# Moving one Gram product behind the chunk outputs, swapping three PSUM banks, and clamping a norm one slot later

## The chip, the cores and the metric

The kernel runs on one core of a Trainium2 chip. The metric is the device time of one execution in microseconds; of several executions the median is taken. TensorE is called PE, VectorE DVE, ScalarE ACT, GpSimd POOL, and the queue that issues most transfers SP.

## The reference

Two transformer-like blocks are applied to a sequence of 512 tokens of width 1024, in float32. The change touches only one part of the first block: a linear recurrence with 8 heads of 64 channels, run forwards and backwards over the tokens.

```python
def rwkv7_scan(r, w, k, v, kk, a, reverse):
    def step(state, inp):
        r_t, w_t, k_t, v_t, kk_t, a_t = inp
        sa = jnp.einsum('bhij,bhj->bhi', state, -kk_t)
        state = (state * w_t[:, :, None, :]
                 + sa[..., None] * (kk_t * a_t)[:, :, None, :]
                 + v_t[..., None] * k_t[:, :, None, :])
        y_t = jnp.einsum('bhij,bhj->bhi', state, r_t)
        return state, y_t
...
    kk = (k * k_k.astype(f32)).reshape(B, S, H, N)
    kk = kk / jnp.maximum(jnp.sqrt(jnp.sum(kk * kk, axis=-1, keepdims=True)), 1e-12)
...
    y = (rwkv7_scan(r_h, decay[:, :, 0], k_dir[:, :, 0], v_h, kk, a[:, :, 0], False)
         + rwkv7_scan(r_h, decay[:, :, 1], k_dir[:, :, 1], v_h, kk, a[:, :, 1], True))
```

Around it stand an input projection, a differential attention, gates, output projections, a feed-forward network, and a whole second block; none of these is edited.

## The kernel before

The recurrence is computed in chunks of 64 tokens, by `rwkv_block`. A pair is 128 channels, so two heads; there are four pairs (`RT = 4`), one after the other, and for each both directions `d` = 0 and 1 are worked on side by side. A pair goes through these stages, in which every engine has its own written-out order:

1. Gram products. `gram_l(p, d)` multiplies within each chunk (32 matmuls) into PSUM: direction 0 into pair 3 (banks 6 and 7), direction 1 into pair 2 (banks 4 and 5). DVE then runs `begin(p, d)`: four instructions (L1363, L1365, L1367, L1369), whose last one gives `X`, on which PE's next stage waits (semaphore `x0`). DVE runs `begin` for direction 0, then for direction 1, and only then the rest.
2. Inversion in five levels by doubling, in banks 0 and 1 (bank `d` for direction `d`). A level has two rounds: PE multiplies (L1090, semaphore `m1`), DVE masks into `E` (L1409), PE multiplies again (L1103, semaphore `px`), ACT copies out (L1273), DVE transposes (L1421). Between the rounds stand slots 0 to 9 of `beside(p, slot)` with other work: on PE the second Gram products of this pair in slots 1 and 2, with their masks on DVE (L1379, L1380), and `prepare(p + 1, n)`, the preparation of the next pair.
3. Right sides, then the run over the chunks: seven steps. A step is two matmuls per direction (L1161) into bank 4 + d, and one DVE instruction per direction (L1451, semaphore `zout`). In the same stretch PE sums those parts of the output that do not need the state (L1170) into banks 0 and 1, and transposes the next pair's operands (L1018).
4. At the end of a pair PE does `gram_l(p + 1, 0)` and `gram_l(p + 1, 1)`, then the output part that needs the states (64 matmuls, L1187, again into banks 1 and 0), and ACT copies the two banks out (L1295, semaphore `yo`). PE waits for both copies before level 1 of the next pair.

Among all this, PE also does 128 tiles of a gate projection in bank 3, three matmuls each (L839, L840, L841). `Gates.STEPS` says how many tiles stand at each point of the order: two at the end of a pair (behind L1187), none at slot 0, two at slot 1, one at slot 2. DVE scales the finished gate tiles (L869) and splits their weights (L854).

The preparation that the second edit touches goes through bank 2 and passes from engine to engine. Step 1: PE sums squares over a head (L985, semaphore `kksum`). Step 2: DVE clamps the sum from below (L1314, semaphore `kkmax`), and PE waits for that before its next product in the same bank (L988, semaphore `lora`), which ACT turns into a sigmoid (L1204) ahead of its next copies L1273. PE has this product at slot 2, behind the second Gram product of direction 1 and ahead of one gate tile and of L1103 of level 2. DVE has the clamp at slot 1:

```python
                    if p + 1 < RT:
                        if slot != 2:
                            prepare(p + 1, slot)
                        if slot == 1:
                            prepare(p + 1, 2)
```

The functions below are printed whole, with the profile's line numbers.

Of the kernel before, what the change touches and what calls it, by code (L numbers as in the profile page):

```python
# [885 lines left out]
def rwkv_block(pr, U, w_lora, room, spare, gates, back, room_free, earlier):  # L886
# [4 lines left out]
    with ExitStack() as ctx:  # L891
# [63 lines left out]
        with nc.Block() as block:  # L955
# [17 lines left out]
            def _(pe):  # L973
# [60 lines left out]
                def gram_l(p, d):  # L1034

                    if d == 0:
                        pe.wait_ge(s["trout"], 6 * p + 5)
                    elif p:
                        pe.wait_ge(s["zout"], 14 * p)
                    gram(p, d, "Bh")  # L1040

                def times_v(p, d):
# [34 lines left out]
                gates.pe(pe, 19)  # L1077
                for p, point in enumerate(pair_points):
                    if p:
                        pe.wait_ge(s["yo"], 2 * p)  # L1080
                    for lev in range(1, 6):
                        u = 5 * p + lev - 1
                        for d, a in both(p):
# [67 lines left out]
                    for i in range(NCH - 1):  # L1151
                        for d, a in both(p):
                            at = ORDER[d][i]
                            if i == 0:
                                pe.wait_ge(s["phiout"], 2 * p + d + 1)
                                pe.wait_ge(s["zero"], 2 * p + d + 1)
                                pe.wait_ge(s["psiout"], 4 * p + 2 * d + 2)
                            else:
                                pe.wait_ge(s["zout"], 14 * p + 2 * (i - 1) + d + 1)
                            for hh in range(2):  # L1160
                                last = nc.tensor.matmul(pr.bank[4 + d][rows64(hh), (i % 4) * 64:(i % 4 + 1) * 64],  # L1161
                                                        a["Phi"][rows64(hh), 4 * (at % 2) + at // 2, :], a["Z"][rows64(hh), at, :],
                                                        start=True, stop=True)
                            last.then_inc(s["step"], 1)
                        for b, hh, d, a, k in fixed_parts[5 * i:5 * (i + 1)]:
                            q, h = hh * TB + b, rows64(hh)
                            for cc in range(2):
                                r = rows64(cc)
                                left, right = ((vN[r, b, h], a["A2"]), (a["N"][r, q, 0:64], a["A1"]))[k]
                                last = nc.tensor.matmul(pr.bank[1 - cc][h, 64 * b:64 * b + 64], left, right[r, q, :],  # L1170
                                                        start=(b == 0 and d == 0 and k == 0), stop=False, skip_group_check=True)
                        if i == 6:
                            last.then_inc(s["fixed"], 1)
                        gates.pe(pe, point + 12 + i)
                        if i and p + 1 < RT:
                            transposes(p + 1, i - 1)
                    if p + 1 < RT:
                        for d in range(2):
                            gram_l(p + 1, d)
                    pe.wait_ge(s["rbout"], 2 * p + 2)  # L1180
                    pe.wait_ge(s["zout"], 14 * p + 14)
                    pe.wait_ge(s["fixed"], p + 1)
                    for b in range(TB):
                        for cc in range(2):
                            for d, a in both(p):
                                for hh in range(2):
                                    last = nc.tensor.matmul(pr.bank[1 - cc][rows64(hh), 64 * b:64 * b + 64],  # L1187
                                                            a["Z"][rows64(hh), 2 * b + cc, :],
                                                            a["Rb"][rows64(hh), (2 * b + cc) * CH:(2 * b + cc + 1) * CH],
                                                            start=False, stop=(d == 1), skip_group_check=True)  # L1190
# [4 lines left out]
            def _(act):  # L1195
# [70 lines left out]
                for p, point in enumerate(pair_points):  # L1266
                    for lev in range(1, 5):
                        u = 4 * p + lev - 1
                        beside(p, 2 * lev - 2)
                        gates.act(act, point + 2 * lev - 2)  # L1270
                        for d, a in both(p):
                            act.wait_ge(s["px"], 2 * u + d + 1)
                            nc.scalar.copy(flat(a["X"][:, :, :]), pr.bank[d]).then_inc(s["xout"], 1)  # L1273
                        beside(p, 2 * lev - 1)
                        gates.act(act, point + 2 * lev - 1)
                    beside(p, 8)
                    gates.act(act, point + 8)
                    for d, a in both(p):
                        act.wait_ge(s["y5"], 2 * p + d + 1)
                        nc.scalar.copy(flat(a["Y64"][:, :, :]), pr.bank[d]).then_inc(s["y64"], 1)  # L1280
                    gates.act(act, point + 9)
                    for d, a in both(p):
                        act.wait_ge(s["n"], 2 * p + d + 1)
                        act.wait_ge(s["gram"], 4 * (p + 1))
                        nc.scalar.mul(a["N"], pr.pair[2 + d][:, :].rearrange("p (q t) -> p q t", q=8), -1.0).then_inc(s["nout"], 1)
                    beside(p, 9)
                    for i in range(10, 13):
                        gates.act(act, point + i)
                    for i in range(6):
                        gates.act(act, point + 13 + i)  # L1290
                        if p + 1 < RT:
                            transposed(p + 1, i)
                    act.wait_ge(s["y"], p + 1)
                    for cc in range(2):
                        nc.scalar.copy(U[:, p, :].rearrange("p (b cc t) -> p b cc t", b=TB, cc=2)[:, :, cc, :],  # L1295
                                       pr.bank[1 - cc][:, 0:256].rearrange("p (b t) -> p b t", b=TB)).then_inc(s["yo"], 1)
                    gates.act(act, point + 19)

            @block.vector
            def _(dve):  # L1300
# [70 lines left out]
                def beside(p, slot):  # L1371
                    if slot == 0:
                        for d, a in both(p):
                            nc.vector.tensor_tensor(by_head(a["A1"][:, :, :]), gram_part(d, 0), by_token(incl, d), ALU.mult)\
                                .then_inc(s["a1"], 1)
                    if slot in (1, 2):
                        d, a = both(p)[slot - 1]
                        dve.wait_ge(s["gram"], 4 * p + slot + 2)
                        nc.vector.tensor_tensor(by_head(a["M"]), gram_part(d, 1), by_token(strict, d), ALU.mult).then_inc(s["m"], 1)  # L1379
                        nc.vector.tensor_tensor(by_head(a["A2"][:, :, :]), gram_part(d, 0), by_token(incl, d), ALU.mult).then_inc(s["a2"], 1)  # L1380
                    if p + 1 < RT:
                        if slot != 2:
                            prepare(p + 1, slot)
                        if slot == 1:
                            prepare(p + 1, 2)
                    if slot == 8:
                        bonus(p)

# [15 lines left out]
                for p, point in enumerate(pair_points):  # L1404
# [40 lines left out]
                    for i in range(NCH - 1):  # L1445
                        for d, a in both(p):
                            at, nxt = ORDER[d][i], ORDER[d][i + 1]
                            dve.wait_ge(s["step"], 14 * p + 2 * i + d + 1)
                            if i == 0:
                                dve.wait_ge(s["psiout"], 4 * p + 2 * d + 2)  # L1450
                            nc.vector.scalar_tensor_tensor(a["Z"][:, nxt, :], pr.bank[4 + d][:, (i % 4) * 64:(i % 4 + 1) * 64],  # L1451
                                                           a["pin"][:, at, CH * (1 - d):CH * (1 - d) + 1], a["Z"][:, nxt, :],
                                                           ALU.mult, ALU.add).then_inc(s["zout"], 1)
                        gates.dve(dve, point + 12 + i)
                        if i == 0:
                            dve.wait_ge(s["rb"], 2 * p + 2)
                            order = "p (b cc t) -> p cc b t"
                            for d, a in both(p):
                                nc.vector.tensor_tensor(a["Rb"].rearrange(order, b=TB, cc=2), a["Rt"].rearrange(order, b=TB, cc=2),
                                                        heads_of(pr.pair[3], 256 * d), ALU.add).then_inc(s["rbout"], 1)  # L1460
# [1541 lines left out]
```

## Time and profile before

| quantity | value |
|---|---|
| median of three executions | 1845.11 us (1844.65 to 1846.07) |
| the profiled execution, its own time | 1846.07 us |
| its span, from the first to the last instruction | 1844.3 us |
| PE busy | 1733.6 us (94%) |
| DVE busy | 1052.2 us (57%) |
| ACT busy | 706.6 us (38%) |
| mean granted PE clock over the span | 0.982 |

The profile is of one execution. The busy time of PE includes the time a matmul takes to pass through, so a busy PE is not PE at its peak. A row of the order of instructions gives the start in the span, the duration, the engine, the source line, the tensors, the shapes and how many instructions were merged into the row; in brackets stand the idle time of the engine before it and what ended that.

### The profile page before, as it was taken

Reading aid. Unit: us, or ns where it says so; the run is one execution under the profiler, and the core shown is the slowest. Engines: PE = TensorE matmul, PEld = TensorE weight load, DVE = VectorE, ACT = ScalarE, POOL = GpSimd, SP = SyncE. Lnnn points to the kernel's source line nnn. Section 1 sums busy time; section 2 is a strip of 40 time slices with the busy share of each in tenths; the row PEclk is TensorE's granted clock in tenths of the full one; section 3 lists DMA queues with packets and bytes.
Section 4 is the critical chain, followed back from the end, with each engine's and each line's share of the span. In section 5 each row is a group of like instructions: output and inputs, shape, how many; then the busy total and the mean of one; then the engine's idle time right before and its main releaser. Section 6 shows DMA issues by size and latency. Waiting matters only on the chain. (4 is left out here: it accounts for less than half of the span.)

```text
span 1844.3 us, 29753 instructions
## 1 busy us (share of the span) xinstructions
PE 1733.6 (94%) x12674; PEld 1357.3 (74%) x12674; DVE 1052.2 (57%) x1461; ACT 706.6 (38%) x1051; POOL 113.4 (6%) x133
## 2 busy tenths in 40 slices
PE   7999789999998999999999989998988899999997
PEld 5666557787886788888888768885466678888885
DVE  6767456665645757767676674226686454343433
ACT  4344433343324444323233534234664334231412
POOL 2000000000000010001111110003100100000001
PEclk9999989999999999999999999999999999999998
DMA  5111220100105434435564131140001222323231
GB/s 202 63 62 61 97 82 30 44 23 33 32 25 206 160 126 157 152 138 194 197 232 144 60 108 49 67 138 13 1 1 36 92 69 92 103 92 103 93 100 49
DMA packets 49156, 171.68 MB, mean 93 GB/s; under 512 B 5552, under 2 KB 6960, under 8 KB 48256
## 3 DMA queue, kind: packets, MB, share of 16 engines
q1 hardware_dynamic: 39184, 133.26, 21.0%
q0 software_dynamic: 9840, 36.51, 5.9%
q8 instruction: 101, 1.65, 0.4%
q14 instruction: 31, 0.25, 0.0%
HBM read 161.10 MB, written 8.65 MB: 92 GB/s over the span
## 5 line engine op out<-in xcount | busy, mean ns | idle before, releaser
L361 PE MATMUL pair<-h_hi,w_hi 128*128 128x512 f32 x1032 | 417.1, 404 | 33.4 <-DVE w_lo L399 15.4
L362 PE MATMUL pair<-h_lo,w_hi 128*128 128x512 f32 x1032 | 405.5, 393 | 0.0
L363 PE MATMUL pair<-h_hi,w_lo 128*128 128x512 f32 x1032 | 405.4, 393 | 0.0
L399 DVE TENSOR_TENSOR w_lo<-w_raw,w_hi 128x1024 fp32r<-128x1024 f32 (+2 forms) x225 | 266.0, 1184 | 212.2 <-ACT w_hi L384 212.1
L384 ACT CAST w_hi<-w_raw 128x1024 fp32r<-128x1024 f32 (+2 forms) x225 | 221.9, 989 | 226.5 <-PE pair L363 223.0
L361 PEld LDWEIGHTS pair<-h_hi,w_hi 128*128 128x128 f32 x1032 | 196.0, 190 | 92.5 <-DVE w_lo L399 31.9
L362 PEld LDWEIGHTS pair<-h_lo,w_hi 128*128 128x128 f32 x1032 | 196.0, 190 | 42.6 <-issue 3.8
L363 PEld LDWEIGHTS pair<-h_hi,w_lo 128*128 128x128 f32 x1032 | 195.8, 190 | 42.0
L361 PE MATMUL pair<-ff_f_hi,w_hi 128*128 128x512 f32 x512 | 199.7, 390 | 0.5 <-DVE w_lo L399 0.5
L362 PE MATMUL pair<-ff_f_lo,w_hi 128*128 128x512 f32 x512 | 199.2, 389 | 0.0
L363 PE MATMUL pair<-ff_f_hi,w_lo 128*128 128x512 f32 x512 | 199.2, 389 | 0.0
L2385 ACT ACTIVATE ff_sq<-ff_relu 128x512 f32<-128x512 f32 x64 | 40.5, 632 | 219.4 <-DVE ff_relu L2414 110.4
L361 PEld LDWEIGHTS pair<-ff_f_hi,w_hi 128*128 128x128 f32 x512 | 96.1, 188 | 20.8 <-DVE w_lo L399 1.0
L363 PEld LDWEIGHTS pair<-ff_f_hi,w_lo 128*128 128x128 f32 x512 | 96.1, 188 | 19.9
L362 PEld LDWEIGHTS pair<-ff_f_lo,w_hi 128*128 128x128 f32 x512 | 96.1, 188 | 19.9
L2417 DVE TENSOR_TENSOR ff_f_lo<-ff_sq,ff_f_hi 128x512 fp32r<-128x512 f32 x64 | 44.4, 693 | 86.5 <-ACT ff_f_hi L2389 86.5
L839 PE MATMUL pair<-h_hi,gate_hi 128*128 128x512 f32 x128 | 61.1, 478 | 16.2 <-DVE w_raw_low L854 14.8
L2425 DVE SCALAR_TENSOR_TENSOR x<-pair,mod,x 128x512 f32<-128x512 f32 x32 | 24.0, 750 | 88.9 <-PE pair L363 88.9
L2286 DVE SCALAR_TENSOR_TENSOR mod_acc<-mod_w,silu_c,mod_acc 128x1024 f32<-128x1024 f32 x56 | 71.5, 1279 | 3.5 <-DMA mod_w<-in_w_mod 3.3
L841 PE MATMUL pair<-h_hi,w_raw_low 128*128 128x512 f32 x128 | 51.9, 405 | 0.0
L840 PE MATMUL pair<-h_lo,gate_hi 128*128 128x512 f32 x128 | 51.6, 403 | 0.0
L741 ACT ACTIVATE norm_sq<-x 128x512 f32<-128x512 f32 x40 | 25.0, 624 | 68.7 <-DVE x L2238 33.7
(422 smaller groups left out, 2543.0 us busy)
## 6 DMA issues: line engine op xcount, KB each, us to landing
w_raw<-in_w_ff SPq DMA_DIRECT2D x128, 512.0 KB, 3.3
mod_w<-in_w_mod POOLq DMA_DIRECT2D x48, 512.0 KB, 3.6
w_raw<-in_w_in SPq DMA_DIRECT2D x22, 512.0 KB, 3.2
w_raw<-in_w_gate SPq DMA_DIRECT2D x16, 512.0 KB, 3.3
w_raw<-in_w_out SPq DMA_DIRECT2D x16, 512.0 KB, 3.3
w_raw<-in_w_rwkv SPq DMA_DIRECT2D x15, 512.0 KB, 3.3
w_raw<-in_w_da SPq DMA_DIRECT2D x12, 512.0 KB, 3.5
g_spill<-norm_pair POOLq DMA_DIRECT2D x16, 256.0 KB, 2.6
```

What stands on the lines that cost most here:

```text
L361: nc.tensor.matmul(out, w_hi, x_hi, start=(k == 0), stop=False)
L362: nc.tensor.matmul(out, w_hi, x_lo, start=False, stop=False)
L363: last = nc.tensor.matmul(out, w_lo, x_hi, start=False, stop=(k == kt - 1))
L384: nc.scalar.copy(hi[:, s % SPLIT_SLOTS, 0:cols], pr.raw[:, w % RAW_SLOTS, 0:cols]).then_inc(pr.hi_made, 1)
L399: nc.vector.tensor_tensor(lo[:, s % SPLIT_SLOTS, 0:cols], pr.raw[:, w % RAW_SLOTS, 0:cols], hi[:, s % SPLIT_SLOTS, 0:cols].bitcast(F32), A ...
L741: nc.scalar.activation(pr.sum_sq[:, k % 2, :], self.x[:, k, :], ACT.Square).then_inc(pr.sum_squared, 1)
L839: nc.tensor.matmul(pr.bank[3], w_hi, x_hi, start=(k == 0), stop=False)
L840: nc.tensor.matmul(pr.bank[3], w_hi, x_lo, start=False, stop=False)
L841: last = nc.tensor.matmul(pr.bank[3], w_lo, x_hi, start=False, stop=(k == KT - 1))
L2286: nc.vector.scalar_tensor_tensor(acc, w, c, acc, ALU.mult, ALU.add).then_inc(self.added, 1)
L2385: nc.scalar.activation(self.sq[:, u % 2, :], self.relu[:, u % 2, :], ACT.Square).then_inc(self.sq_made, 1)
L2417: nc.vector.tensor_tensor(self.f_lo[:, g % 2, j, :], self.sq[:, u % 2, :], self.f_hi[:, g % 2, j, :].bitcast(F32), ALU.subtract)\
```

## The change

It has three edits.

- The step of direction 1 goes to bank 0 instead of bank 5, and the output sums go to banks 5 and 1 instead of 1 and 0.
- `gram_l(p + 1, 1)`, which writes banks 4 and 5, moves from ahead of L1187 to the beginning of the next pair. There it stands behind the two gate tiles and waits for both copies of the output (`yo`) instead of for the last step (`zout`); the wait that stood there is now inside it. It happens at three places, between pairs 0 and 1, 1 and 2, 2 and 3.
- DVE clamps the sum (preparation step 2) at slot 2, behind the two masks of that slot, instead of at slot 1. It happens in pairs 0, 1 and 2. The order of PE and of ACT in this preparation stays.

```diff
                     if d == 0:
                         pe.wait_ge(s["trout"], 6 * p + 5)
                     elif p:
-                        pe.wait_ge(s["zout"], 14 * p)
+                        pe.wait_ge(s["yo"], 2 * p)
                     gram(p, d, "Bh")
...
                 for p, point in enumerate(pair_points):
                     if p:
-                        pe.wait_ge(s["yo"], 2 * p)
+                        gram_l(p, 1)
...
-                                last = nc.tensor.matmul(pr.bank[4 + d][rows64(hh), (i % 4) * 64:(i % 4 + 1) * 64],
+                                last = nc.tensor.matmul(pr.bank[4 - 4 * d][rows64(hh), (i % 4) * 64:(i % 4 + 1) * 64],
...
-                                last = nc.tensor.matmul(pr.bank[1 - cc][h, 64 * b:64 * b + 64], left, right[r, q, :],
+                                last = nc.tensor.matmul(pr.bank[5 - 4 * cc][h, 64 * b:64 * b + 64], left, right[r, q, :],
...
                     if p + 1 < RT:
-                        for d in range(2):
-                            gram_l(p + 1, d)
+                        gram_l(p + 1, 0)
...
                     if p + 1 < RT:
-                        if slot != 2:
-                            prepare(p + 1, slot)
-                        if slot == 1:
-                            prepare(p + 1, 2)
+                        prepare(p + 1, slot)
```

L1187 and the reader L1295 change their bank in the same way as L1170, and the reader L1451 in the same way as L1161.

## Rows read from the trace of the kernel before

**Rows 1.** The page: busy time of each engine.

```profile
PE 1733.6 (94%) x12674; PEld 1357.3 (74%) x12674; DVE 1052.2 (57%) x1461; ACT 706.6 (38%) x1051; POOL 113.4 (6%) x133
```

**Rows 2.** Windows over the recurrence: busy time of PE, PEld, DVE, ACT, POOL, granted clock.

```profile
282.00:568.00 286.00, 271.52 (x5940) 222.85 (x5929) 173.44 (x311) 92.91 (x139) 6.66 (x13) 0.99 0.13 45
```

**Rows 3.** Order of instructions on PE from the first pair to the second.

```profile
352.86 1.98 PE L1030 MATMUL pair<-rw_rkb 64*64 64x128 f32 x64
354.65 2.04 PE L1187 MATMUL pair<-rw_kh,rw_e 64*64 64x64 f32 x64
356.63 0.50 PE L839 MATMUL pair<-h_hi,gate_hi 128*128 128x512 f32 x1
...
358.21 1.15 PE L1090 MATMUL pair<-rw_x,rw_lc 64*64 64x64 f32 x32
359.75 1.15 PE L1090 MATMUL pair<-rw_x,rw_lc 64*64 64x64 f32 x32 [0.39 <-DVE rw_x L1369]
```

**Rows 4.** The same stretch on DVE and ACT.

```profile
354.03 0.69 DVE L1363 TENSOR_TENSOR rw_lc<-pair,rw_masks 128x512 f32<-128x512 f32 x1 [2.14 <-PE pair L1030]
...
356.84 0.65 DVE L1363 TENSOR_TENSOR rw_lc<-pair,rw_masks 128x512 f32<-128x512 f32 x1
...
358.98 0.71 DVE L1369 STREAM_TRANSPOSE rw_x<-rw_y 128x512 f32<-128x512 f32 x1
...
360.95 0.69 DVE L1409 TENSOR_TENSOR rw_e<-pair,rw_masks 128x512 f32<-128x512 f32 x1 [0.68 <-PE pair L1090]
...
356.73 0.65 ACT L1295 COPY rwkv_in<-pair 128x256 f32<-128x256 f32 x2 [3.19 <-PE pair L1187]
```

**Rows 5.** The first L1363 of the third and of the fourth pair on DVE.

```profile
427.71 0.69 DVE L1363 TENSOR_TENSOR rw_lc<-pair,rw_masks 128x512 f32<-128x512 f32 x1 [2.14 <-PE pair L1030]
...
501.36 0.69 DVE L1363 TENSOR_TENSOR rw_lc<-pair,rw_masks 128x512 f32<-128x512 f32 x1 [2.14 <-PE pair L1030]
```

**Rows 6.** Order of instructions on DVE, slots 1 and 2 of the second pair.

```profile
369.40 0.68 DVE L1314 TENSOR_SCALAR norm_sq<-pair 128x512 f32<-128x512 f32 x1
370.25 0.69 DVE L1409 TENSOR_TENSOR rw_e<-pair,rw_masks 128x512 f32<-128x512 f32 x1 [0.18 <-PE pair L1090]
...
372.71 0.68 DVE L1380 TENSOR_TENSOR rw_ma<-pair,rw_masks 128x512 f32<-128x512 f32 x1
373.30 1.21 DVE L854 TENSOR_TENSOR w_raw_low<-w_raw,gate_hi 128x1024 fp32r<-128x1024 f32 x1
375.71 0.71 DVE L1421 STREAM_TRANSPOSE rw_y<-rw_x 128x512 f32<-128x512 f32 x1 [1.20 <-ACT rw_x L1273]
```

**Rows 7.** The same slots on PE and ACT.

```profile
371.95 1.12 PE L988 MATMUL pair<-rwkv_in,w_lora 64*128 64x512 f32 x2
...
373.90 2.08 PE L1103 MATMUL pair<-rw_e,rw_y 64*64 64x64 f32 x64
...
373.11 0.69 ACT L1204 ACTIVATE x<-pair,params 128x512 f32<-128x512 f32 x1 [4.70 <-PE pair L988]
375.10 0.59 ACT L1273 COPY rw_x<-pair 128x512 f32<-128x512 f32 x1 [1.30 <-PE pair L1103]
```

**Rows 8.** The clamp and the product behind it in pair 0's own preparation.

```profile
245.32 0.69 DVE L1314 TENSOR_SCALAR norm_sq<-pair 128x512 f32<-128x512 f32 x1 [0.17 <-PE pair L985]
...
246.06 1.12 PE L988 MATMUL pair<-rwkv_in,w_lora 64*128 64x512 f32 x2 [0.78 <-DVE norm_sq L1314]
```

**Rows 9.** L1314 over the whole span, and slot 2 of the last pair on DVE.

```profile
L1314 DVE TENSOR_SCALAR norm_sq<-pair x4: 675/675/692, 245.3 to 443.1; 128x512 f32<-128x512 f32 x4
...
514.05 0.69 DVE L1409 TENSOR_TENSOR rw_e<-pair,rw_masks 128x512 f32<-128x512 f32 x1 [0.90 <-PE pair L1090]
```

**Rows 10.** Output product of the last pair; windows (columns as Rows 2) there and in slot 0.

```profile
561.89 3.42 PE L1187 MATMUL pair<-rw_kh,rw_e 64*64 64x64 f32 x64 [0.38 <-DVE rw_e L1451]
...
562.00:563.00 1.00, 1.00 (x21) 1.00 (x23) 0.00 (x0) 0.00 (x0) 0.00 (x0) 0.50 0.14 41
...
365.00:366.00 1.00, 0.00 (x0) 0.00 (x0) 0.00 (x0) 0.99 (x2) 0.00 (x0) 1.00 0.00 0
```

More of the change, by code:

```diff
@@ L1186, in _ @@
                                 for hh in range(2):
-                                    last = nc.tensor.matmul(pr.bank[1 - cc][rows64(hh), 64 * b:64 * b + 64],
+                                    last = nc.tensor.matmul(pr.bank[5 - 4 * cc][rows64(hh), 64 * b:64 * b + 64],
                                                             a["Z"][rows64(hh), 2 * b + cc, :],
@@ L1295, in _ @@
                         nc.scalar.copy(U[:, p, :].rearrange("p (b cc t) -> p b cc t", b=TB, cc=2)[:, :, cc, :],
-                                       pr.bank[1 - cc][:, 0:256].rearrange("p (b t) -> p b t", b=TB)).then_inc(s["yo"], 1)
+                                       pr.bank[5 - 4 * cc][:, 0:256].rearrange("p (b t) -> p b t", b=TB)).then_inc(s["yo"], 1)
                     gates.act(act, point + 19)
@@ L1450, in _ @@
                                 dve.wait_ge(s["psiout"], 4 * p + 2 * d + 2)
-                            nc.vector.scalar_tensor_tensor(a["Z"][:, nxt, :], pr.bank[4 + d][:, (i % 4) * 64:(i % 4 + 1) * 64],
+                            nc.vector.scalar_tensor_tensor(a["Z"][:, nxt, :], pr.bank[4 - 4 * d][:, (i % 4) * 64:(i % 4 + 1) * 64],
                                                            a["pin"][:, at, CH * (1 - d):CH * (1 - d) + 1], a["Z"][:, nxt, :],
```

## The prediction

> **What bounds the kernel now.** The page comes first [rows 1]. PE is busy 1733.6 us of 1844.3, so in most stages its work sets the time. The edits lie in the recurrence, though, so I read that stage by itself. The windows from 282 to 568 us give PE 271.5 us of 286.0 and DVE 173.4 [rows 2], 14.5 us without work on PE. An average cannot say who waits for whom, so the order of instructions is the view that decides. I read it at the two places that are edited.
>
> At the end of a pair [rows 3, 4] the reader is to see that DVE sets the pace, although PE looks full. PE starts the 64 Gram matmuls at 352.86. DVE begins direction 0 at 354.03, direction 1 at 356.84 with no idle time between, and ends at 358.98 + 0.71 = 359.69. PE has by then done the output product, two gate tiles and the first L1090. Its second L1090 starts at 359.75, after 0.39 us of waiting for DVE's L1369. That is the chain: Gram product of direction 0, eight instructions on DVE, second L1090, L1409. The third and fourth pair begin in the same way [rows 5]: DVE has waited 2.14 us each time, and the first L1363 stand 73.68 and 147.33 us behind the one at 354.03.
>
> At slot 2 it is PE that is dense [rows 6, 7]: L988 at 371.95, a gate tile, L1103 at 373.90. ACT and DVE wait for PE there, ACT 1.30 us ahead of L1273, DVE 1.20 us ahead of L1421. DVE did the clamp L1314 at 369.40, ending at 370.08, 1.87 us before PE needs it. It then still waited 0.18 us for PE.
>
> **The change part by part.**
>
> *The banks.* The numbers of instructions, their shapes and the engines stay. I cost the swap at nothing: step, sum and reader go to other banks, and nothing is queued differently for it. A price per instruction has no row of before. It can be bounded from L1187: 64 of them take 2.04 us in banks 0 and 1 [rows 3], and the same 64 took 3.42 us only at half clock [rows 10]. A bank effect of even 5% on that product would be 0.1 us a pair. I keep ±0.4 us over four pairs in the range.
>
> *The moved Gram product (A).* What it takes away ahead of the output product is half of the 64 matmuls. By L1187's start these last 354.65 - 352.86 = 1.79 us, so half is 0.89. The output product then starts at 353.76, the gate tiles at 356.63 - 0.89 = 355.74, and PE comes to the beginning of the pair at 358.21 - 0.89 = 357.32. The new wait for the copies costs nothing: L1295 started 0.04 us after the product had ended and ran 0.65 us [rows 4], so it now ends at 356.73 + 0.65 - 0.89 = 356.49, 0.83 us before PE asks. If that cover were gone, each microsecond over it would be added. Then come the 32 matmuls of direction 1, and the first L1090 stands at 358.21 as before, because PE has the same work in another order.
>
> DVE pays. From the start of a Gram product to the DVE instruction that it releases it was 354.03 - 352.86 = 1.17 us [rows 3, 4]. So the L1363 of direction 1 starts at 357.32 + 1.17 = 358.49 instead of 356.84, 1.65 us late. Nothing can be pulled into the gap: DVE's next own instruction, the L1409 of direction 0, stands behind `begin` of direction 1 in its queue. The second L1090 moves from 359.75 to 361.40, L1409 from 360.95 to 362.60. Behind it in DVE's queue stand the gate scaling, the masks A1 and the next pair's norm, for which ACT waits. PE's following products stand behind the late L1090. So the whole kernel is late by the 1.65 us. Bounds: a different hand-over between the two products on PE could make it 1.5, a slower release 1.8. I take 1.65. Three places give 3 x 1.65 = 4.95 us.
>
> *The clamp one slot later (B).* In slot 1 DVE loses 0.68 us of work and gains nothing, for L1409 at 370.25 had been waiting for PE's L1090 [rows 6]. In the last pair, which has no clamp, the same L1409 came after 0.90 us of idle time instead of 0.18 [rows 9]. In slot 2 DVE does L1409 twice and both masks at their old times, because the Gram product that they need is ahead of L988 on PE. The clamp then takes the place of L854, at 373.30. From the start of a clamp to the start of the L988 that waits for it a row gives 246.06 - 245.32 = 0.74 us [rows 8], with clamps of 0.69 us there and 0.675 us in the median [rows 9]. L988 thus starts at 374.04 instead of 371.95: 2.09 us late.
>
> Queued behind L988 on PE are a gate tile and L1103, on ACT the sigmoid L1204 ahead of both L1273, and on DVE both L1421. None of them has slack against PE: L1273 had waited 1.30 us for L1103. The pushed L854 ends 0.6 us later, at 375.1, inside DVE's old wait that ended at 375.71, so that part is free; it would cost up to 0.6 us if that wait were gone. PE's products from 371.95 to L1103 and past it are back to back, so there is no hole that takes up the 2.09 us. Bounds: 1.9 (a quicker release) and 2.7 (L854 no longer covered). I take 2.09. Three pairs give 6.27 us.
>
> *The clock.* Both edits open a hole in PE's work, of 0.39 + 1.65 = 2.04 us at the second L1090 and of 2.09 us at L988. The granted clock is 1.00 where PE has nothing at all to do from 365 to 366 us, and 0.50 at 562 us, late in the last pair [rows 10]. So the sum takes full speed. The Trainium skill speaks against the change here: "TensorE: Matmul & The Clock Gate", Part 1, calls the low clock (1.2 GHz) the default, and has activity release it and idleness bring it back. By that rule the new holes could cost more than their own length. This trace agrees that the clock falls within the stage, to 0.50 at 562 us, but shows no fall at the hole of slot 0. With the rule the sum would be the clock rival's below, without it the sum here.
>
> **Sum.** 4.95 + 6.27 = 11.2 us. The profiled execution took 1846.07 us, a span of 1844.3 and 1.8 around it; it becomes 1857.3, with a span of 1855.5. It lies 0.96 us over the median of the three runs, 1845.11, so the median becomes 1856.3. The two delays add, since A is paid before level 1 and B in level 2 of the same pair, one after the other in PE's order. Everything behind the recurrence starts when it ends and moves along; I found no transfer in it that is bound to a fixed time.
>
> **Rivals.**
>
> 1. *The clock falls* at the new holes. For it: two holes of 2 us in 15 us, with the one of slot 0 between them. Against it: clock 1.00 there now. Price from the one product at both clocks: 3.42 - 2.04 = 1.38 us for one such product at the low clock. Once per hole is 6 x 1.38 = 8.3 us more, 1864.6; at three of the holes it is 1860.4.
> 2. *Only one of the two delays reaches the end.* The other would be taken up by a wait that I read as following PE but which hangs on something else, as a chain of preparation from the pair before. With A alone 1845.1 + 4.95 = 1850.1, with B alone 1851.4. For it: PE does have 14.5 us without work in the stage. Against it: most of these are waits for DVE and ACT work that starts from the very products that come late.
> 3. *PE, not DVE, sets the pace at the end of a pair* (other side). The output product, its copies and the gate tiles end 0.89 us earlier. If the next pair hung on those, this would be a gain of up to 3 x 0.89 = 2.7 us, and, with the clamp hidden in DVE's idle time, 1842.4. It decides once DVE is done with direction 1 before PE's first L1090 has run. DVE is now 0.39 us later than that, and A makes it later, not earlier. It also needs B at nothing, against the dense PE rows.
> 4. *The edits do nothing measurable*: both delays are absorbed, 1845.1. It would need 2 us of slack behind L988, and the rows show none.
>
> **Numbers.** The forecast case 0.78, the clock 0.08, one delay only 0.08, no change 0.03, the other side 0.03. The forecast case by itself runs from 3 x (1.5 + 1.9) = 10.2 to 3 x (1.8 + 2.7) = 13.5 us, with ±0.4 for banks and ±0.7 for the scatter of a median (the three runs span 1.4 us): 1854.2 to 1859.7. The low end reaches half way to the one-delay case, 1853.2, the high end takes in the mild clock case, 1860.4. A change within 0.2% (3.7 us) cannot be told from none. Slower by more than that: 0.78 + 0.08 + 0.08 = 0.94, minus a little for errors of reading that I cannot name: 0.93. Within 0.2%: 0.04. Faster: 0.03.
>
> **What would show it.** On the way into pairs 1, 2 and 3, DVE's second L1363 with about 1.6 us idle time put down to PE's L1030, and PE's second L1090 with about 2.0 us idle time put down to L1369. At slot 2 of pairs 0 to 2, L988 with about 2.1 us idle time put down to L1314. First L1363 of successive pairs 73.7 + 1.65 + 2.09 = 77.4 us apart. Clock 1.00 at the new holes, and the last L1187 about 11 us later than at 561.89. Step A would be wrong if L1363 of direction 1 started without a wait, step B if L988 did, or if the waits were there and the distance between pairs stayed at 73.7. The forecast fails if the clock falls, or if a wait behind level 2 shrinks by what L988 grows.

## The result and the profile after

The changed kernel takes 1861.20 us in the median of four executions (1860.28 to 1862.27), the kernel before 1845.59 us (four, 1844.65 to 1846.22). The ratio is 1.0085, with a 95% interval of 1.0067 to 1.0103: 15.6 us slower. The forecast was 11.2 us slower, 1856.3, with a range from 1853.2 to 1860.4. All medians below are of executions at the usual clock; the one that is left out is an execution of g2 that took 2514.44 us at a mean clock of 0.745.

The profile is of a further execution of the changed kernel (1861.23 us). Its page shows nearly the same busy times as [rows 1], in a span of 1859.4 us instead of 1844.3:

```profile
PE 1740.4 (94%) x12674; PEld 1363.4 (73%) x12674; DVE 1052.9 (57%) x1461; ACT 706.4 (38%) x1051; POOL 113.4 (6%) x133
```

PE did the same 12674 matmuls in 6.8 us more busy time. That is the first sign that more than waiting was added.

In the changed kernel's source the lines behind the edit stand a few lines further up: L1362 is the former L1363, L1368 is L1369, L1313 is L1314, and L1186 is L1187. L1090, L1030, L988 and L1103 kept their numbers. The order of instructions from the first pair to the second, PE first and then DVE and ACT, answers to [rows 3, 4]:

```profile
354.47 1.10 PE L1030 MATMUL pair<-rw_rkb 64*64 64x128 f32 x32
355.39 2.04 PE L1186 MATMUL pair<-rw_kh,rw_e 64*64 64x64 f32 x64
...
358.95 1.10 PE L1030 MATMUL pair<-rw_rkb 64*64 64x128 f32 x32
359.88 1.11 PE L1090 MATMUL pair<-rw_x,rw_lc 64*64 64x64 f32 x32
363.07 1.15 PE L1090 MATMUL pair<-rw_x,rw_lc 64*64 64x64 f32 x32 [2.08 <-DVE rw_x L1368]
...
355.64 0.69 DVE L1362 TENSOR_TENSOR rw_lc<-pair,rw_masks 128x512 f32<-128x512 f32 x1 [2.14 <-PE pair L1030]
...
360.12 0.69 DVE L1362 TENSOR_TENSOR rw_lc<-pair,rw_masks 128x512 f32<-128x512 f32 x1 [1.59 <-PE pair L1030]
...
357.47 0.65 ACT L1294 COPY rwkv_in<-pair 128x256 f32<-128x256 f32 x2 [2.31 <-PE pair L1186]
```

From DVE's first L1362 to its second it is 360.12 - 355.64 = 4.48 us, where it was 356.84 - 354.03 = 2.81 [rows 4]: 1.67 us more, against the forecast 1.65. DVE waits 1.59 us for the moved Gram product, and PE's wait ahead of its second L1090 grew from 0.39 to 2.08 us. The output copies end at 358.12, 0.83 us before the moved product starts, so the new wait for them costs nothing.

Slot 2 of the second pair answers to [rows 6, 7], DVE first:

```profile
376.02 0.68 DVE L1379 TENSOR_TENSOR rw_ma<-pair,rw_masks 128x512 f32<-128x512 f32 x1
376.62 0.68 DVE L1313 TENSOR_SCALAR norm_sq<-pair 128x512 f32<-128x512 f32 x1
...
377.36 1.12 PE L988 MATMUL pair<-rwkv_in,w_lora 64*128 64x512 f32 x2 [2.02 <-DVE norm_sq L1313]
378.41 0.50 PE L839 MATMUL pair<-h_hi,gate_hi 128*128 128x512 f32 x1
378.75 0.58 PE L840 MATMUL pair<-h_lo,gate_hi 128*128 128x512 f32 x1
379.12 0.63 PE L841 MATMUL pair<-h_hi,w_raw_low 128*128 128x512 f32 x1
379.68 3.21 PE L1103 MATMUL pair<-rw_e,rw_y 64*64 64x64 f32 x64
```

L988 waits for the clamp for 2.02 us, as forecast. The last two lines were not forecast. L841 takes 0.63 us where it took 0.40 before, and the 64 matmuls of L1103 take 3.21 us instead of 2.08 [rows 7]. The windows of the changed kernel (columns as Rows 2) show the reason in the column before the last two:

```profile
300.00:304.00 4.00, 4.00 (x76) 3.72 (x76) 0.71 (x1) 0.82 (x3) 0.00 (x0) 0.57 0.00 0
365.00:369.00 4.00, 4.00 (x83) 3.80 (x86) 2.14 (x4) 1.81 (x2) 0.54 (x1) 0.57 0.19 72
379.00:383.00 4.00, 4.00 (x76) 3.35 (x77) 0.68 (x1) 0.85 (x3) 0.00 (x0) 0.60 0.00 0
444.00:448.00 4.00, 4.00 (x81) 3.34 (x84) 2.13 (x4) 1.82 (x2) 0.54 (x1) 0.62 0.17 66
458.00:461.00 3.00, 3.00 (x45) 2.32 (x45) 0.00 (x0) 0.27 (x2) 0.00 (x0) 0.55 0.00 0
522.00:526.00 4.00, 4.00 (x94) 4.00 (x94) 3.10 (x5) 0.79 (x2) 0.54 (x1) 0.57 0.17 66
```

The granted clock falls to 0.5 (1.2 instead of 2.4 GHz) behind each of the six new holes: behind L988 in pairs 0 to 2 (300, 379, 458 us), and behind the second L1090 in pairs 1 to 3 (365, 444, 522 us). In the kernel before it was 1.00 in all those places. A seventh fall, at the last output product (577 us), is not new: the kernel before has it too [rows 10]. The Trainium skill has it in "TensorE: Matmul & The Clock Gate", Part 1, that idleness brings the low clock back. This trace agrees, with six falls for six holes. The idle stretches that the page speaks of are longer than the 2.0 to 2.1 us here, and the measurement decides.

**Lengths of the pairs.** The cleanest measure in all traces below is the time from the first L1363 of one pair to that of the next. For pair 3 it is the time to the first output copy (L1295). "Stage" is their sum. All are worked out from starts in the order of instructions, in us:

| kernel | pair 0 | pair 1 | pair 2 | pair 3 | stage |
|---|---|---|---|---|---|
| before | 73.65 | 73.68 | 73.65 | 63.99 | 284.97 |
| before, again (e9) | 73.67 | 73.64 | 73.69 | 61.82 | 282.82 |
| changed | 77.30 | 78.99 | 79.13 | 66.73 | 302.15 |
| changed, again (e7) | 75.76 | 78.81 | 80.30 | 64.86 | 299.73 |
| e1 Gram moved, old banks | 73.65 | 76.56 | 75.58 | 64.93 | 290.72 |
| e2 Gram moved, new banks | 73.64 | 75.39 | 75.38 | 66.99 | 291.40 |
| e3 clamp moved | 77.25 | 75.76 | 77.30 | 64.46 | 294.77 |
| e4 clamp ahead of the masks | 74.28 | 74.27 | 74.44 | 62.29 | 285.28 |
| e5 both holes filled | 76.21 | 77.47 | 77.45 | 63.02 | 294.15 |
| e6 Gram ahead of the gate tiles | 73.69 | 73.63 | 73.86 | 62.13 | 283.31 |
| e8 hole at L988 filled | 75.89 | 77.49 | 78.72 | 63.77 | 295.87 |
| f1 norm first | 71.88 | 71.88 | 71.91 | 63.85 | 279.52 |
| g1 Gram moved, norm first | 71.89 | 76.66 | 74.06 | 65.83 | 288.44 |
| g2 changed, norm first | 75.47 | 78.69 | 78.70 | 67.11 | 299.97 |

Pair 3 also scatters for two reasons that are not the edits': a fall of the clock at the last output product (it is in the first trace of before, not in e9), and 0 to 1.9 us of idle PE ahead of the last step (L1161), for which the traces name no releaser.

The stage of the changed kernel is 17.2 us longer than before's. It also begins 2.0 us earlier in the span, so that the whole is 15.2 us longer. Ahead of the stage the profiled execution of before ran at a low clock for some time, which the changed kernel's did not. The windows of the kernel before (columns as Rows 2) show it:

```profile
270.00:275.00 5.00, 3.62 (x16) 2.86 (x16) 3.70 (x6) 2.12 (x3) 0.54 (x1) 0.66 0.42 150
```

The same window of the changed kernel:

```profile
270.00:275.00 5.00, 4.01 (x26) 3.25 (x25) 2.80 (x4) 3.19 (x5) 0.54 (x1) 1.00 0.22 85
```

That fall belongs to the execution and not to the kernel: the second execution of before (e9) has none there, and the second of the changed kernel (e7) has one.

### The profile page after: what moved, and what is told of

Read it like the earlier page. It is cut to its first block and busy times, and to the rows that moved or that the text cites. A ratio compares the mean times of both kernels' runs of the same rounds, so it can differ in the third digit from the quotient of the medians.

```text
span 1859.4 us, 29750 instructions
## 1 busy us (share of the span) xinstructions
PE 1740.4 (94%) x12674; PEld 1363.4 (73%) x12674; DVE 1052.9 (57%) x1461; ACT 706.4 (38%) x1051; POOL 113.4 (6%) x133
## 3 DMA queue, kind: packets, MB, share of 16 engines
q8 instruction: 101, 1.65, 0.4%
## 5 line engine op out<-in xcount | busy, mean ns | idle before, releaser
L841 PE MATMUL pair<-h_hi,w_raw_low 128*128 128x512 f32 x128 | 51.9, 406 | 0.0
```

The source lines that it names most:

```text
L841: last = nc.tensor.matmul(pr.bank[3], w_lo, x_hi, start=False, stop=(k == KT - 1))
```

## The experiments

Each edit is against the kernel before or the changed one, as said. "Before" in the results is the kernel before, run on the same chip in the same session.

**Which edit costs what (e1, e2, e3).** e1 takes the moved Gram product alone, with the old banks. e2 is the changed kernel with the clamp put back into slot 1. e3 moves only the clamp.

```diff
# e1, against before
-                        pe.wait_ge(s["zout"], 14 * p)
+                        pe.wait_ge(s["yo"], 2 * p)
...
-                        pe.wait_ge(s["yo"], 2 * p)
+                        gram_l(p, 1)
...
-                        for d in range(2):
-                            gram_l(p + 1, d)
+                        gram_l(p + 1, 0)
# e3, against before
-                        if slot != 2:
-                            prepare(p + 1, slot)
-                        if slot == 1:
-                            prepare(p + 1, 2)
+                        prepare(p + 1, slot)
```

> Direction 1's Gram product alone moved behind the output product, its copies and the gate tiles; all banks as before, clamp in slot 1 as before. Theory of waits and clock: DVE idles 1.6 us ahead of its second L1363 of pairs 1 to 3, that is 3 x 1.66 = 5.0 us; if the granted clock falls behind these holes, L1103 behind them runs slower, but in pairs 1 and 2 ACT's table load hides it, and only pair 3 pays up to 1 us: 1850.6 to 1851.6 against 1845.6. Rival, the banks carry the cost: no more than 1 us over before.

> The same move with the new banks, clamp in slot 1 as before. Theory of waits and clock: the same time as the move with the old banks, within 0.5 us. Rival, the banks cost something (or the copies from bank 5 come late): 2 to 4 us more than with the old banks, seen in longer L1161, L1170 or copies.

> Only the clamp moved to slot 2. Theory of waits and clock: L988 idle 2.0 us in pairs 0 to 2 (6.1 us), and behind each hole the granted clock is 0.50 for some microseconds, which costs 1.6 us each: 10.5 to 11 us, 1856.3. Rival, the clock falls only where both holes stand in one pair: it falls nowhere or once, 6 to 8 us, 1851.7 to 1853.5.

Measured: e1 1851.67 us (ratio 1.0034, interval 1.0022 to 1.0047), e2 1853.08 us (1.0040, 1.0028 to 1.0053), e3 1853.89 us (1.0049, 1.0036 to 1.0062), before 1845.09 us. Both halves cost. e1 and e2 differ by 1.4 us in time, more than the 0.5 us expected but within their intervals, and the pairs do not show a price of the banks: where the clock fell for a similar time, pair 2 lasts 75.58 with the old and 75.38 with the new banks, and a matmul of L1161 and of L1170 has a median of 218 ns in both.

e3 came out 2 us below its expectation, and its trace shows the clock's price well, for in that execution it fell behind two of the three holes only. The order of instructions on PE in e3, pair 0 and pair 1:

```profile
299.67 1.12 PE L988 MATMUL pair<-rwkv_in,w_lora 64*128 64x512 f32 x2 [2.02 <-DVE norm_sq L1314]
301.87 3.34 PE L1103 MATMUL pair<-rw_e,rw_y 64*64 64x64 f32 x64
...
376.91 1.12 PE L988 MATMUL pair<-rwkv_in,w_lora 64*128 64x512 f32 x2 [2.02 <-DVE norm_sq L1314]
378.86 2.08 PE L1103 MATMUL pair<-rw_e,rw_y 64*64 64x64 f32 x64
```

The windows behind L988 in pairs 0, 1 and 2:

```profile
300.00:304.00 4.00, 4.00 (x45) 2.61 (x45) 0.75 (x1) 0.79 (x2) 0.00 (x0) 0.66 0.00 0
377.00:381.00 4.00, 4.00 (x77) 2.83 (x79) 1.31 (x2) 1.29 (x3) 0.00 (x0) 1.00 0.00 0
455.00:459.00 4.00, 4.00 (x92) 4.00 (x88) 0.91 (x2) 1.17 (x2) 0.00 (x0) 0.59 0.00 0
```

The wait is the same 2.02 us. With the clock at 1.00, pair 1 is 75.76 - 73.65 = 2.11 us longer. That is the wait alone, forecast as 2.09. With the fall, pairs 0 and 2 are 3.60 and 3.65 longer. A fall behind L988 thus costs 1.5 us.

**How often a hole brings a fall.** Over all traces that have holes of 2.0 to 2.1 us, the clock fell behind 26 of 33 of them: changed 6 of 6, e1 3 of 3, e2 3 of 3, e3 2 of 3, e7 3 of 6, e8 2 of 3, g1 1 of 3, g2 6 of 6. It fell behind none of the 24 holes of 1.8 us ahead of L985 in the same stage, and behind none of the twelve waits of 0.5 to 0.6 us in e4 and behind the fillers of e5 and e8. No run varied the length of one hole between 1.8 and 2.0 us, so whether the length or the place makes that difference is not shown.

**Is it the idle PE that lowers the clock (e5, e8)?** Useless matmuls fill the holes of the changed kernel. They read a table of ones and a constant table and write a free bank. e8 has only the first half of the diff.

```diff
+                    if slot == 2 and p + 1 < RT:
+                        pe.wait_ge(s["a2"], 2 * p + 1)
+                        for n in (512, 256):
+                            nc.tensor.matmul(pr.bank[7][:, 0:n], c["head_ones"], keep[:, 0:n], start=True, stop=True)
                     if slot < 6 and p + 1 < RT:
                         prepare(p + 1, slot)
...
                             if lev == 1:
+                                if p and d:
+                                    pe.wait_ge(s["trout"], 6 * (p + 1))
+                                    for n in (512, 256):
+                                        nc.tensor.matmul(pr.bank[2][:, 0:n], c["head_ones"], keep[:, 0:n], start=True, stop=True)
                                 pe.wait_ge(s["x0"], 2 * p + d + 1)
```

> The changed kernel with useless matmuls on PE in both holes (128x128 by 128x512 and 128x256 in float32 ahead of L988 in pairs 0 to 2, and ahead of the second L1090 of pairs 1 to 3); their results are not used. Theory of waits and clock: PE's waits shrink from 2.0 to about 0.5 us, the granted clock stays 1.00 in the recurrence, and although PE does more the kernel is 5 to 6 us faster than the changed one: 1855.5. Rival, the time above the sum of the two waits is not the clock's: 1861 or more.

> The changed kernel with the useless matmuls only ahead of L988, not ahead of the second L1090. Theory of waits and clock: the clock stays full behind L988 and still falls behind the second L1090; in pairs 1 and 2 that is hidden behind ACT, so those pairs last as with both holes filled (77.4 to 77.5 us from L1363 to L1363), and only the last pair is 1 us longer. Rival, the fall behind the second L1090 costs time in pairs 1 and 2 too: these last 78.5 us or more.

Measured: e5 1858.44 us (ratio 1.0070, 1.0057 to 1.0084; before 1845.09), e8 1858.86 us (1.0080, 1.0065 to 1.0095; before 1844.29). In e5 L1092 and L1063 are the fillers, and L1098 and L1111 the former L1090 and L1103. The order of instructions on PE:

```profile
358.98 1.56 PE L1092 MATMUL pair<-norm_sq,consts 128*128 128x512 f32 x4
361.12 1.15 PE L1098 MATMUL pair<-rw_x,rw_lc 64*64 64x64 f32 x32 [0.59 <-DVE rw_x L1376]
...
373.31 1.56 PE L1063 MATMUL pair<-norm_sq,consts 128*128 128x512 f32 x4
375.40 1.12 PE L988 MATMUL pair<-rwkv_in,w_lora 64*128 64x512 f32 x2 [0.54 <-DVE norm_sq L1321]
...
377.35 2.08 PE L1111 MATMUL pair<-rw_e,rw_y 64*64 64x64 f32 x64
```

The window over the recurrence:

```profile
282.00:568.00 286.00, 273.62 (x5812) 220.68 (x5810) 170.00 (x303) 91.64 (x135) 6.48 (x12) 1.00 0.10 35
```

PE's waits are 0.5 to 0.6 us, the clock is 1.00 over the recurrence, and L1111 takes 2.08 us again. With more work on PE the stage became 8.0 us shorter, 294.15 instead of 302.15. Not all of that is the fillers': pair 3 gave 3.7 us, and part of it is the fall at the last output product, which comes and goes in the kernel before too. In pairs 0 to 2 alone it is 235.42 - 231.13 = 4.3 us, against e7 3.7 us. Against the second trace of before, whose stage also ran at full clock, e5's stage is 294.15 - 282.82 = 11.3 us longer: near the forecast sum of the two waits, with the clock taken out. The parts fit less well than the sum. Pairs 1 and 2 are 3.8 us longer, as the waits say, but pair 0 is 2.5 us longer instead of 2.1, and pair 3 is 1.2 instead of 1.7. In pair 3 e9 has 0.46 us of idle PE ahead of the last step and e5 none; for pair 0 the runs give no reason.

The kernel's time did not follow in full: it is 2.8 us below the changed kernel's, not 5 to 6, and so between the theory and its rival. The rest came back behind the stage. There ACT in e5 waits for the gates' reload:

```profile
575.62 1.66 ACT L384 CAST w_hi<-w_raw 128x512 fp32r<-128x512 f32 x3 [3.33 <-PEq L215]
577.29 1.28 ACT L2158 ACT_TABLE_LOAD   x1
580.55 1.67 ACT L2158 ACTIVATE gates<-gates 128x512 f32<-128x512 f32 x3 [1.98 <-DMA gates<-g_spill]
```

From the first copy of the last output to the end of the span it was 1286.3 us here, 1279.0 before. Of these 7.3 us some 5 have come by the end of the reload's work, and 1.6 more behind a fall of the clock at 647 us, which neither the changed kernel nor the one before has in its trace. e9 bears the first part out: its last pair is 2.2 us shorter than before's, ACT then waits 1.91 us for the reload, and the stretch to the end is 2.1 us longer (1281.1). So what the last pair saves by the clock is lost again at the reload. By the source the reload waits for the store of the last gate tile; no run changed that.

e8 falls between its theories. The clock fell twice, behind the second L1090 of pairs 2 and 3. In pair 2 it stayed low from 439 to 446 us, and the pair took 78.72 us, 1.2 more than pair 1 with no fall (77.49). So a fall in slot 0 is not always hidden behind ACT. The short ones in e2 were: its pairs 1 and 2 are 1.7 us longer than before, no more than the wait, though L1103 took 3.26 us in pair 1 and 2.99 in pair 2. The long one in e1's pair 1 was not, 76.56 against 75.58.

**Where in the slot the clamp stands (e4), and which part of the move costs (e6).** e4 puts the clamp into slot 2, but ahead of the two masks. e6 puts the Gram product behind the output product, but ahead of the gate tiles. Both are against before.

```diff
# e4
+                    if slot == 2 and p + 1 < RT:
+                        prepare(p + 1, 2)
                     if slot in (1, 2):
...
                         if slot != 2:
                             prepare(p + 1, slot)
-                        if slot == 1:
-                            prepare(p + 1, 2)
# e6
-                        for d in range(2):
-                            gram_l(p + 1, d)
+                        gram_l(p + 1, 0)
...
                     last.then_inc(s["y"], 1)
+                    if p + 1 < RT:
+                        gram_l(p + 1, 1)
                     gates.pe(pe, point + 19)
```

> Only the clamp moved to slot 2, but ahead of that slot's two masks instead of behind them. Theory of waits and clock: the clamp starts 0.6 us after L1409's second start, L988 waits some 0.6 us instead of 2.0, the hole is too short to lower the granted clock, and a pair grows by 0.6 us: 3 x 0.6 = 1.8 us, 1846.9. Rival, any move of the clamp behind L1409 costs the whole of B with its clock: 10 us.

> Direction 1's Gram product behind the output product but ahead of the two gate tiles, banks as before, clamp as before. Theory of waits: PE reaches it at 355.7 instead of 357.3, DVE gets it 1.2 us later, at about the time at which it has done direction 0, so the pair grows by 0.1 us and the kernel by 0.3 us or less: 1845.1 to 1845.4. Rival, it is the output product ahead of it that costs: 1 us or more a place.

Measured: e4 1846.06 us (ratio 1.0004, 0.9995 to 1.0012), e6 1845.99 us (1.0000, 0.9991 to 1.0009), before 1845.19 us. In e4 PE waits a quarter as long and L1103 keeps its length:

```profile
372.38 1.12 PE L988 MATMUL pair<-rwkv_in,w_lora 64*128 64x512 f32 x2 [0.52 <-DVE norm_sq L1314]
374.33 2.08 PE L1103 MATMUL pair<-rw_e,rw_y 64*64 64x64 f32 x64
```

Its pairs are 0.6 to 0.8 us longer, as expected, and no fall stands in the recurrence. In the medians that is 0.9 us, no clear difference from before. So of the 2.1 us and the fall, 0.6 us come from the slot. The rest comes from the two masks of 0.6 us each that stand ahead of the clamp in the changed kernel. In e6 DVE goes from direction 0 to direction 1 (L1370 and L1364 there) without a wait:

```profile
355.84 0.71 DVE L1370 STREAM_TRANSPOSE rw_x<-rw_y 128x512 f32<-128x512 f32 x1
356.48 0.65 DVE L1364 TENSOR_TENSOR rw_lc<-pair,rw_masks 128x512 f32<-128x512 f32 x1
```

Its pairs 0 to 2 are as long as before's to 0.2 us. The output product ahead of the Gram product costs nothing; the gate tiles ahead of it, 1.6 us on PE, are what DVE waits for.

**Does it repeat (e7, e9)?**

> The changed kernel once more, on the chip of these runs. Theory of waits and clock: the waits come out the same to 0.1 us (1.59 us at L1362 of direction 1, 2.0 us at L988), and only where and for how long the clock is low differs from the first trace: 1860 to 1862. Rival, the waits themselves scatter: they differ by more than 0.3 us.

> The kernel before once more, for a second trace. Theory of waits and clock: the pairs last 73.65 us again, with full clock in pairs 0 to 2; what differs between executions of it is a fall of the clock ahead of the recurrence or behind it: 1843 to 1846.5. Rival, falls of the clock inside pairs 0 to 2 occur in the kernel before too and the first trace had none by luck.

Measured: e7 1861.06 us (ratio 1.0083, 1.0069 to 1.0097; before 1845.19); e9 1843.65 us, one execution. The waits repeat, 1.59 us at each second L1362 and 2.02 at L988. The falls do not: e7 has three in its six holes, against six in the first trace. Its pair 0 has none and is 2.11 us longer than before; pair 2 has two, one of them long, and lasts 80.30. Almost the same median, 1861.06 against 1861.20, thus comes of different sets of falls. The kernel before had no fall in pairs 0 to 2 in either trace, and in e9 none in the whole stage.

**A kernel faster than both (f1), and the change on top of it (g1, g2).** Before L985 PE is idle for 1.8 us in slot 0, because ACT's square and table load start only when DVE has done the gate scaling, both masks A1 and L1311. f1 lets DVE do L1311 first. g1 adds to f1 the moved Gram product with its new banks, g2 the whole change.

```diff
-                        if slot != 2:
+                        if slot not in (0, 2):
                             prepare(p + 1, slot)
...
+                        if lev == 1 and p + 1 < RT:
+                            prepare(p + 1, 0)
                         if lev in (1, 5):
                             gates.dve(dve, point + 2 * lev - 2)
```

> The kernel before with one thing else: DVE does the next pair's first step (L1311) right behind level 1's second L1409, ahead of the gate scaling and the two masks A1, in pairs 0 to 2. ACT's square, table load and sigmoid then start 1.8 us earlier, and PE's hole of 1.8 us ahead of L985 closes: 3 x 1.6 to 1.8 = 5 us less, 1840.2. Rival, PE waits there for the masks A1 or the copies instead: 0 to 2 us less.

> The moved Gram product with its new banks, clamp in slot 1, and the next pair's first step (L1311) brought forward on DVE, which takes the hole ahead of L985 away. Theory of waits and clock: 1838.5 + 3 x 1.7 = 1843.6 if the one hole that is left in slot 0 does not lower the clock; where it falls there, ACT no longer hides it and each fall costs up to 1.5 us: up to 1848. Rival, bringing L1311 forward also takes up the wait of the moved Gram product: 1840 or less.

> The whole change with L1311 brought forward. Theory of waits and clock: 1838.5 + 3 x 1.7 + 3 x 2.1 = 1849.9 at full clock, and 1854 to 1856 if the clock falls behind the holes ahead of L988 and of the second L1090 as in the changed kernel. Rival, the falls need the hole ahead of L985 between the two others: 1850.

Measured: f1 1838.53 us (ratio 0.9961, 0.9948 to 0.9973; before 1845.19), faster than both kernels. The order on DVE in f1:

```profile
357.00 0.69 DVE L1409 TENSOR_TENSOR rw_e<-pair,rw_masks 128x512 f32<-128x512 f32 x1 [0.68 <-PE pair L1090]
357.60 0.48 DVE L1311 TENSOR_SCALAR rw_kk<-rwkv_in,params 128x512 f32<-128x512 f32 x1
357.99 0.69 DVE L869 TENSOR_TENSOR norm_pair<-pair,norm_rstd 128x512 f32<-128x512 f32 x1
```

The pairs are 73.65 - 71.88 = 1.77 us shorter, all of the hole; that makes 5.3 us, and the time is 6.7 us lower, with 5.3 still inside the interval. g1 took 1849.39 us (1.0028, 1.0018 to 1.0038; before 1844.29), 10.9 us above f1, where the waits explain 5.1 and the expectation went to 1848. In the traces the stage is 8.9 us longer than f1's, of which a single fall, in pair 1, makes 3.1; the rest of the difference of the medians is not explained. In its profiled pair 1 the low clock fell on the second L1090 and all that follows. It lasted 76.66 us, 3.1 more than f1's 71.88 and the wait of 1.7. The window:

```profile
360.00:367.00 7.00, 7.00 (x106) 5.38 (x103) 3.75 (x7) 3.20 (x5) 0.54 (x1) 0.52 0.11 41
```

g2 took 1858.97 us (1.0082, 1.0065 to 1.0099). It was expected at 1854 to 1856 with the falls, so this expectation was 3 us low. Its pair 1 is 71.88 + 1.7 + 2.1 = 75.68 and 3.0 us more for two falls, so both are paid in full. Its pair 2 is the same, and pair 0, with one fall, is 1.5 above 71.88 + 2.1. Without the hole ahead of L985 as cover, a fall in slot 0 costs as much as one behind L988. The falls also do not need the hole ahead of L985, which is gone here.

## Why the prediction was wrong

*What bounds the stage* held. At the end of a pair DVE set the pace, at slot 2 PE did: each of the two new waits appeared where it was forecast, and what stands behind it came later.

*The banks at nothing* held: e1 and e2 have pairs of the same length to 0.2 us, where the falls are alike.

*A, 1.65 us at three places,* held: 1.67 us on DVE, and pairs 1.7 us longer in e2. e6 adds that it is the gate tiles ahead of the Gram product that make it.

*B, 2.09 us in three pairs,* held: 2.11 us in the pairs of e3 and e7 that ran at full clock. The two waits also add, and everything behind them moves along: e5's stage at full clock is 11.3 us longer than e9's, against a forecast of 11.2.

*The clock* is the step that failed. The falls were put at nothing: "So the sum takes full speed." I had taken it from one idle microsecond at clock 1.00 in slot 0 of the kernel before. Those rows gave no ground for the new holes: the hole of 1.8 us brought no fall in any of 24 cases, holes of 2.0 to 2.1 us brought one in 26 of 33. The forecast's own list of what would break it had this first ("The forecast fails if the clock falls"). The mechanism was rival 1, to which I had given 0.08. Its price of 1.38 us for one product was near the 1.5 us measured behind L988. In the first trace the falls made the rest of the stage, 17.2 - 3 x 1.7 - 3 x 2.1 = 5.8 us: 1.5, 1.5 and 1.7 us in pairs 0 to 2, and 1.0 us in pair 3. In the medians the part above the two waits is 15.6 - 11.4 = 4.2 us. Rival 1's milder version, falls at three holes, gave 1860.4, near the measured 1861.2. That is in part luck: in the first trace four of the six falls were paid for, 5.8 us together, and e7 came to the same time with three falls at partly other places.

*The fall behind the second L1090* stood in rival 1 at the full 1.38 us. That it can be hidden was not in the prediction in any form: in pairs 1 and 2 PE's wait ahead of L985 shrinks from 1.79 us to 0.3 us in exchange, as these rows of the changed kernel and of the one before show:

```profile
369.95 1.10 PE L985 MATMUL pair<-norm_sq,consts 128*128 128x512 f32 x2 [0.29 <-ACT x L1203]
...
366.63 1.10 PE L985 MATMUL pair<-norm_sq,consts 128*128 128x512 f32 x2 [1.79 <-ACT x L1204]
```

The fall is paid in pair 3, which has no such wait, and where the low clock lasts long. Up to the first L1161 of pair 3 it was 54.9 to 55.3 us in the five traces with the fall, 53.9 to 54.2 in the three without (e5, e7, g1).

What stays open is why a given hole brings a fall in one execution and none in the next: e3's three holes are alike in length and surroundings.

## What to carry to other kernels

Price a new wait on a dense TensorE twice, by its length and by what the engine does behind it if its clock falls, and count on the second price. Full clock behind one hole as long is no proof that the next one is free: e3's three holes are alike, and two brought a fall. When an instruction moves on a queue, look at what it then stands behind: the clamp cost 0.6 us a pair ahead of two masks and 2.1 to 3.6 us behind them, the Gram product nothing ahead of two gate tiles and 1.7 us behind them. Start a chain that leaves through another engine ahead of work that nobody waits for yet: f1 gained 6.7 us by one DVE instruction moved up.

## What the runs showed of the hardware

More matmuls can make a stage shorter. With 1.56 us of useless matmuls in each of six holes the granted clock stayed at 1.00 behind all six, where it had been 0.5. Pairs 0 to 2, which hold five of the holes, went from 235.42 to 231.13 us.

Idle stretches of TensorE of 2.0 to 2.1 us in this stage were followed by the low clock in 26 of 33 cases, and the same kernel had it six times in one execution and three times in another.

How much a low clock costs depends on where it falls: 1.5 us behind L988, nothing in slot 0 of e2's pairs 1 and 2, 3.1 us in g1's pair 1.
